# Experts in blocks of 32 slots, four side by side on TensorE, with the overflow blocks fetched by bounded row numbers on GpSimd's queue

## The reference, cut to what matters

```python
def hier_moe(h, router_g, router_g_b, router_e, router_e_b, w_gate, w_up, w_down):
    # 4 groups of 8 experts; each token takes the best group, and in it the best two experts
    ...
    for gi in range(N_EXPERT_GROUPS):
        hid = silu(einsum('td,edf->tef', xt, w_gate[gi])) * einsum('td,edf->tef', xt, w_up[gi])
        hid = hid * gates[:, gi, :, None]          # zero for the experts that a token does not take
        out = out + einsum('tef,efd->td', hid, w_down[gi])
```

## Time and profile before

| | |
|---|---|
| three runs | 3567.9, 3570.92, 3587.31 us, median 3570.92 |
| the profiled execution | 3579.16 us, span 3577.4, mean granted clock of PE 0.956 |
| busy in the span | PE 3245.1 us (91%), PEld 2503.2 (70%), DVE 1469.1 (41%), ACT 1129.8 (32%), POOL 220.7 (6%) |
| DMA | 623.97 MB, mean 174 GB/s; 494.01 MB on SP's queue, 126.46 MB on POOL's |
| transfers of expert weights | 234 on SP's queue |

### The profile page before, as it was taken

How to read it: one execution, slowest core, us unless ns; L and a number is a source line. 1 busy time by engine, 2 the same in 40 slices (tenths; PEclk the granted TensorE clock), 3 DMA queues, 4 the chain that set the end, 5 groups by cost and what they waited for, 6 DMA issues and landing times. The chain is left out here.

```text
span 3577.4 us, 54626 instructions
## 1 busy us (share of the span) xinstructions
PE 3245.1 (91%) x23980; PEld 2503.2 (70%) x23980; DVE 1469.1 (41%) x2737; ACT 1129.8 (32%) x1805; POOL 220.7 (6%) x370
## 2 busy tenths in 40 slices
PE   7888886999899689997999988999989998888898
PEld 5777675454698554545777766777767876777898
DVE  5455555222344642225323244333253334435554
ACT  4344443121343332113222223222232223224443
POOL 0122220000000000000000101000100000000000
PEclk8899897999999989998999989999999999999999
DMA  6433322999566049992453413444322222213452
GB/s 251 136 106 111 132 97 101 405 421 421 226 242 224 10 187 421 421 398 94 153 182 136 165 55 136 147 180 155 124 94 88 95 88 93 101 36 106 144 192 101
DMA packets 106718, 623.97 MB, mean 174 GB/s; under 512 B 11760, under 2 KB 14320, under 8 KB 48112
## 3 DMA queue, kind: packets, MB, share of 16 engines
q1 hardware_dynamic: 72208, 494.01, 36.1%
q0 software_dynamic: 34272, 126.46, 10.0%
HBM read 619.37 MB, written 1.05 MB: 173 GB/s over the span
## 5 line engine op out<-in xcount | busy, mean ns | idle before, releaser
L347 PE MATMUL ps<-t,t 128*128 128x512 f32 (+1 forms) x3488 | 1223.8, 351 | 113.0 <-DVE t L541 53.2
L348 PE MATMUL ps<-t,t 128*128 128x512 f32 (+1 forms) x3488 | 1212.4, 348 | 0.0
L349 PE MATMUL ps<-t,t 128*128 128x512 f32 (+1 forms) x3488 | 1211.0, 347 | 0.0
L324 DVE TENSOR_TENSOR t<-t,t 128x1024 fp32r<-128x1024 f32 x448 | 549.4, 1230 | 781.7 <-ACT t L305 781.6
L347 PEld LDWEIGHTS ps<-t,t 128*128 128x128 f32 x3488 | 669.3, 192 | 222.5 <-issue 70.3
L349 PEld LDWEIGHTS ps<-t,t 128*128 128x128 f32 x3488 | 669.3, 192 | 85.8
L348 PEld LDWEIGHTS ps<-t,t 128*128 128x128 f32 x3488 | 670.1, 192 | 81.6
L305 ACT ACTIVATE t<-t 128x1024 fp32r<-128x1024 f32 x448 | 469.6, 1054 | 590.0 <-PE ps L349 581.5
L1315 PE MATMUL ps<-t,t 128*64 128x512 f32 x1248 | 301.8, 597 | 8.8 <-DMA t<-in_experts_dram 8.8
L1315 PEld LDWEIGHTS ps<-t,t 128*64 128x64 f32 x1248 | 114.6, 137 | 187.2 <-issue 160.8
L679 POOL DMA_DIRECT2D t<-in_wmod_dram x224 | 118.5, 534 | 1855.9 <-PE ps L628 1738.4
(11 more groups left out here) (307 smaller groups left out, 3121.3 us busy)
## 6 DMA issues: line engine op xcount, KB each, us to landing
t<-in_experts_dram SPq DMA_DIRECT2D x234, 1024.0 KB, 13.5
t<-in_wall_dram SPq DMA_DIRECT2D x221, 1024.0 KB, 4.9
t<-in_wmod_dram POOLq DMA_DIRECT2D x224, 512.0 KB, 5.7
t<-in_wmod_dram SPq DMA_DIRECT2D x16, 512.0 KB, 13.1
t<-in_wall_dram SPq DMA_DIRECT2D x10, 512.0 KB, 3.6
t<-in_lora_dram POOLq DMA_DIRECT2D x8, 512.0 KB, 4.0
t<-in_rcst_dram POOLq DMA_DIRECT2D x1, 1536.0 KB, 6.4
t<-in_x_dram SPq DMA_DIRECT2D x1, 1024.0 KB, 8.1
```

The lines of the kernel that those rows point to most:

```text
L324: e.tensor_tensor(lo, self.raw(n), hi, ALU.subtract).then_inc(*net.wlo.up((self.name, n)))
L347: e.matmul(out, lh, rh, start=start, stop=False, **kw)
L348: e.matmul(out, lh, rl, start=False, stop=False, **kw)
L349: return e.matmul(out, ll, rh, start=False, stop=stop, **kw)
```

## The change

A block has 32 slots, four blocks make a **quad**, and there are 12 quads: near quads 0 to 7 (experts 4q to 4q+3) and far quads 8 to 11 with fifteen far blocks, 32 to 46, since more can be beyond 32 than beyond 64. They are worked on in the order 0, 1, 8, 2, 3, 9, 4, 5, 10, 6, 11, 7 (`ORDER`). PE works on a quad's four blocks side by side, in 32 columns each. Gate and up are done in two halves with other work between, and down of a quad comes behind the first half of the next. The gather is for two quads at a time, 256 columns.

The near transfers stay on SP's queue. `MORE` is 6 instead of 4: the first ten transfers have ten rooms, and after that the near ones go round six (the ring and t_143, t_144). The far blocks have t_139 to t_142 for their own. They are fetched on POOL's queue by `indirect_dma_start`: for each of the 128 partitions DVE has worked out a row number of the expert array (384 per expert), and a row number above the bound is dropped without an error. For a far block that holds nothing the counted expert is 32, whose rows are all above the bound. `min(…, 31)` and `fetch_ids` are gone.

```diff
+MORE = 6
...
+            self.rooms[NS + j], self.turn[NS + j], self.gates[NS + j] = ap, len(self.slots) - 1 + (j + 1) / (MORE + 1), stage
...
-    PAIRS = 20
-    BLOCKS = 39
+    ORDER = (0, 1, 8, 2, 3, 9, 4, 5, 10, 6, 11, 7)
+    QUADS = 12
+    BLOCKS = 47
...
+        turns = [(m, s) for n in range(self.QUADS + 1) for m, s in ((n, 0), (n - 1, 2), (n, 1)) if 0 <= m < self.QUADS]
+        near = 0
+        for n, s in turns:
+            for t, x in enumerate(self.blocks(n)):
+                key = ("moe", layer, "weights", n, s)
+                if x >= 32:
+                    self.w[n, t, s] = net.drawn_slot(t, more[t], ("block", x - 32, s), net.sums, key)
+                else:
+                    if near == NS + MORE:
+                        net.fewer_rooms(4, MORE - 4)
+                    self.w[n, t, s] = net.slot(("expert", 96 * layer + 3 * x + s), SW, net.sums, key)
+                    near += 1
...
+    def pe_gate_up(self, e, w, n, s):
...
+        for k in range(4 * s, 4 * s + 4):
...
+            for t in range(len(self.blocks(n))):
+                w.wait_ge(*net.landed(self.w[n, t, s]))
+                c = 128 * (n % 2) + 32 * t
+                m = e.matmul(net.ps[32 * t:32 * t + 32, b, :], self.Ug[g % 2][:, k, c:c + 32],
+                             net.ring_at(self.w[n, t, s])[:, 512 * (k % 4):512 * (k % 4) + 512], start=(k == 0), stop=(k == 7))
+        m.then_inc(*self.up(net.sums, "weights", n, s))
...
+        for n in range(self.QUADS):
+            g, kk = n // 2 + 1, 2 * (n % 2)
+            self.pe_gate_up(e, w, n, 0)
+            if n:
+                self.pe_down(e, w, n - 1)
+            if g < 6:
+                self.pe_gather(e, w, g, kk, 3)
+            if n:
+                self.pe_scatter(e, w, n - 1)
...
+            self.pe_gate_up(e, w, n, 1)
+            if g < 6:
+                self.pe_gather(e, w, g, kk + 1, 3)
...
+            self.pe_turn(e, w, n, 3 if g < 6 else 0)
...
+        for n in range(self.QUADS):
+            if self.ORDER[n] < 8:
+                continue
+            for s in range(3):
+                for t in range(len(self.blocks(n))):
+                    room, ap, _, _, (_, x, _), (marks, key), _ = net.slots[self.w[n, t, s]]
+                    w.wait_ge(*marks.of(key))
+                    e.indirect_dma_start(ap, None, rows, bass.IndirectOffsetOnAxis(ap=self.ids[:, 3 * x + s:3 * x + s + 1], axis=0),
+                                         bounds_check=12288 * self.l + 12287, oob_is_err=False).then_inc(net.s_drawn[t], 16)
```

More of the change, by code:

```diff
@@ L724, in __init__ @@
         self.rooms = {x: self.ring[:, SW * x:SW * x + SW] for x in range(NS)}
-        self.turn, self.filled, self.freed, self.gates = [x - NS for x in range(NS)] + [0] * NS, [0] * (2 * NS), {}, {}
+        self.turn, self.filled, self.freed, self.gates = [x - NS for x in range(NS)] + [0] * MORE, [0] * (NS + MORE), {}, {}
+        self.drawn = [0] * 4
         self.cst = self.take(NC_)
@@ L814, in more_rooms, with drawn_slot, fewer_rooms @@
         for j, ap in enumerate(aps):
-            self.rooms[NS + j], self.turn[NS + j], self.gates[NS + j] = ap, len(self.slots) + j, stage
-    def fewer_rooms(self):
-        self.rooms = {x: self.rooms[x] for x in range(NS)}
+            self.rooms[NS + j], self.turn[NS + j], self.gates[NS + j] = ap, len(self.slots) - 1 + (j + 1) / (MORE + 1), stage
+    def drawn_slot(self, x, ap, what, marks, key):
+        i, room = len(self.slots), NS + x
+        self.slots.append((room, ap, self.drawn[x], SW, what, self.freed[room], None))
+        self.drawn[x] += 1
+        self.freed[room] = (marks, key)
+        return i
+    def fewer_rooms(self, first=0, n=0):
+        self.rooms = {x: ap for x, ap in self.rooms.items() if x < NS or NS + first <= x < NS + first + n}
     def ring_at(self, i):
@@ L1215, in __init__ @@
         net.top = net.arena
-        more = [f(SW) for _ in range(4)]
+        more = [f(SW) for _ in range(MORE)]
         self.Uf = net.XW[:, :, 256:512]
@@ L1252, in __init__, with blocks, rows @@
         self.w = {}
[L1253 to L1257, removed]
-        net.fewer_rooms()
[L1260 to L1270, removed]
+        turns = [(m, s) for n in range(self.QUADS + 1) for m, s in ((n, 0), (n - 1, 2), (n, 1)) if 0 <= m < self.QUADS]
[5 more added lines that the diff above has]
+                    self.w[n, t, s] = net.drawn_slot(t, more[t], ("block", x - 32, s), net.sums, key)
+                else:
+                    if near == NS + MORE:
+                        net.fewer_rooms(4, MORE - 4)
+                    self.w[n, t, s] = net.slot(("expert", 96 * layer + 3 * x + s), SW, net.sums, key)
+                    near += 1
+        net.fewer_rooms()
+    def blocks(self, n):
+        q = self.ORDER[n]
+        return [x for x in range(4 * q, 4 * q + 4) if x < self.BLOCKS]
+    def rows(self, n):
+        return slice(0, 32 * len(self.blocks(n)))
     def c(self, name):
@@ L1299, in pe_gather @@
         w.wait_ge(*self.of(net.vecs, "tokens low"))
[L1300 to L1318, removed]
@@ L1320, in pe_turn @@
-    def pe_turn(self, e, w, p):
-        net, n = self.net, 64 * len(self.blocks(p))
-        b = self.take(w, 0, "turn", p)
-        w.wait_ge(*self.of(net.vecs, "hidden", p))
+        for j in range(2):
+            f = slice(256 * kk + 128 * j, 256 * kk + 128 * j + 128)
+            out = net.ps[:, b, 256 * j:256 * j + 256]
+            for i in range(2):
+                e.matmul(out, self.Uth[:, i, f], G[:, i, :], start=(i == 0), stop=False)
+                m = e.matmul(out, self.Utl[:, i, f], G[:, i, :], start=False, stop=(i == 1))
@@ L1433, in act, with act_down @@
+        self.emptied(net.acts, ("gather", g, kk), "gather", g, kk)
+    def act_down(self, e, w, n):
+        net, r = self.net, self.rows(n)
+        w.wait_ge(*self.of(net.sums, "weights", n, 2))
+        e.activation(self.Yh[r, :], net.ps[r, 1:3, :], ACT.Copy).then_inc(*self.up(net.acts, "down high", n))
     def act(self, e, w):
@@ L1559, in dve_choice @@
[L1559 to L1566 removed]
+            w.wait_ge(*self.of(net.sums, "gather", g - 2, 3))
```

274 lines of the change are left out of this document (146 added, 128 removed).

## The result

The changed kernel takes 3539.24 us (median of 4, 3533.29 to 3544.3), the kernel before 3577.18 beside it: a ratio of 0.9893, interval 0.9856 to 0.9929. So it is faster, by 38 us and not by the 75 forecast; the direction was right and the size was not. The profiled executions differ by 45.9 us (3577.4 to 3531.5 of span).

A forecast was written before the change was run, and what follows sets the result against it. It took PE and DMA to be equally full in the two MoE loops. Loops of 271 us gain 33 and 36, plus 2 x 3 ahead of them: 75 us less, 3496 against the median, range 3460 to 3530 (60%).

The forecast's parts named there:

- Bounds now: Two MoE loops, 304.1 and 306.9 us: PE and DMA both full, 14.9 us a pair each, so both must shrink.
- Bytes: Transfers per layer: 117 before (291 us), 96 after (239 us), because far blocks hold nothing and their dropped rows move nothing.
- PE four side by side: Matmuls in the loops: four blocks take about as long as two, 3.5 us a group, 14.8 a quad, 178 a loop.
- The group of near transfers: Four rooms released by one increment, six near rooms: 11.0 or 13.0 us a group, mean 12.0, 21.5 groups, 258 us.
- rival (b): Low clock in every near group: 14.5 us a group, 324 a loop, kernel slower at 3602 us; chance 9%.
- Pool: Far-room loads: four issues of 0.9 us plus 2.4 to landing, 6.0; 0.5 us open four times, 2 a loop.
- Rival (c): Pool's issues are dear, x us each: 3554 us at x = 2.0, 3624 at 3.1; chance 13%.
- Head and ahead of the loop: Loop start: ten transfers already there, first group 3.5 us; ahead of it, halved gather columns save about 3 us per layer.
- Tail: Loop end: from the last landing through down to the end of the scatter, 7.2 us.
- Sum: Loop 271 us, gains 33 and 36, plus 2 x 3 ahead of the loops: 75 us in all.

The follow-up runs named there:

- n4: The kernel before with its seven far blocks not fetched and PE's instructions the same: 3569.3 us, ratio 0.9984 to the kernel before.
- n2: The changed kernel without Pool's transfers, near stream going round all ten rooms, far matmuls reading the resident x: 3421.7 us, ratio 0.956 to the kernel before.
- n1: The changed kernel without Pool's 90 indirect transfers, far matmuls reading what the rooms last held, six near rooms kept: 3512.9 us, ratio 0.9818 to the kernel before.
- n10: The changed kernel with the old order of rooms at a layer's start, so six further rooms are not filled first: 3563.3 us, ratio 0.9956 to the kernel before.
- n5: The changed kernel with 384 taken off the far blocks' row numbers, so unused blocks really move rows: 3812.7 us, ratio 1.0655 to the kernel before.
- n3: The changed kernel with near transfers cut into 512 KB halves, each group of four halves released separately, Pool's transfers kept: 3527.1 us, ratio 0.9851 to the kernel before.
- n6: The changed kernel with near transfers in 512 KB halves and no transfers on Pool's queue: 3461.1 us, ratio 0.9676 to the kernel before.
- n7: The changed kernel with near transfers in halves and Pool branching over its transfers when no far block is in use: 3453.4 us, ratio 0.9653 to the kernel before.

## Why the prediction was right or wrong

**Bounds now: right.** Both engines had to be relieved; n4 shows that fewer bytes alone are not enough. The other half, a shorter PE alone, was not tried.

**Bytes: right.** SP's queue fell from 494.01 to 449.96 MB, 42 transfers of 1.0486 MB, and with ten rooms they pass at 2.55 us each (10.2 a group). Nothing of the far blocks moved.

**PE four side by side: right.** 32 records take 3.64 us at the full clock in the timeline (at 780.76, for one), 3.5 forecast (half of the timeline's 7.3; by the 0.242 us a record that the prediction has beside it, two blocks would take 7.7 and not 7.3), and PE's work in the loops fell from 296 to 234 us although most groups wait. The 178 us that the prediction added up for PE are not reached: even in n2 PE is busy 202.

**The group of near transfers: right in form, the term too small, and the larger part of the miss.** Without Pool (n1) the loops give (283.2 - 10.7) / 21.5 = 12.7 and 12.4 us a group for 12.0. With 21.5 groups a loop that is 23 us over the two loops (561.2 for 538). The clock was put well: of the 28 groups that stand in n1's timeline behind a wait for a near transfer, 15 took 4.7 to 6.6 us for their matmuls and the others 3.6 or less, as the prediction's half and half; the granted clock of n1's loops is 0.90 and 0.93. The rule of the Trainium skill that every burst shorter than the DMA wait ahead of it starts at the low clock ("TensorE: Matmul & The Clock Gate", HAM oscillation — how this bites in real kernels) agrees with these 15 of 28 groups and no more; fully applied it was rival (b), 14.5 us a group, and no loop has that. What the 12.0 left out seem to be late landings: the third and fourth matmul sets of the group shown lie 3.84 us apart for 2.49. In the trace's packet records one of the sixteen DMA engines finished 0.6 to 1.5 us behind the fifteen others in ten groups of n1's layer 0, 11.5 us in all, and in nine of the ten a 16 KB packet of code (0.9 to 1.0 us on one engine) had started 2 to 4 us earlier. These 11.5 us are most of the 14 that this loop is over its 269. With ten rooms the same late packets are there (up to 1.5 us behind the others in n2) and the group still takes 10.2 us, so a full queue seems to hide what a queue that runs dry in each group pays. This was read from records and not tested; whether the packets of code are the cause stays open.

**Pool: the step whose working failed.** I took 0.9 us an issue, a release-to-landing of 6.0 us, 0.5 us open at each of four places, 2 us a loop. n1 puts the price at 8.9 a loop, 17.8 for both (26 by the medians). The 6.0 was too small in three places. An issue takes 0.99 us, but four in a row come 1.30 apart, and the first comes 0.8 us or more after the release. A group that found the DMA engines idle shows both:

```profile
675.60 3.62 PE L1336 MATMUL ps<-t,t 128*32 128x512 f32 x26 [0.64 <-DMA t<-in_experts_dram,t]
680.01 0.99 POOL L1742 DMA_INDIRECT t<-in_experts_dram,t  x1 [9.11 <-PE ps L1336]
...
683.89 0.99 POOL L1742 DMA_INDIRECT t<-in_experts_dram,t  x1 [0.30 <-issue]
```

PE is done at 679.2, the fourth issue follows at 683.9 and lands 2.1 us later: 6.8 us for 6.0, with nothing in the way. The third place is the landing, because often something is in the way: the same order of releases frees near rooms and far rooms side by side. Of the 66 transfers whose landing the semaphore records give in full, 22 found the DMA engines less than 30% busy with near packets until they landed, and took 2.1 us from issue to landing (median; 3.5 at most). Another 35 found them at least 70% busy, and took 3.3 to 7.7, median 5.5. I had added the 2.4 us of an idle queue. What I should have asked is what stands ahead of a transfer on the DMA engines, not only on Pool's instruction queue; that the packets were to be tiny made me put the way at its shortest. Rival (c) named Pool's waits with a dear issue as the cause. It cannot be ruled out as a part: its own formula with x = 1.30 gives 4 x (2 x (5.2 + 2.4) - 13) = 8.8 us a loop, which is the size measured. No run parts the two, spacing and late landings; the wait to 770.73 above, where the fourth transfer was issued at 762.96, needs the late landing. None of the 90 issues took over 1.30 us. The Trainium skill's five times longer Pool DMA beside a DVE copy ("SBUF — State Buffer", A bandwidth-pool intuition that's wrong) shows in no issue here: three direct transfers were issued beside a DVE copy and took 0.58 us at most, and none of the indirect ones was.

**Head and ahead of the loop: right.** 6.6 us for 6 ahead of the loops; n10 gives the transfers fetched ahead at 24 us.

**Tail: small miss.** From the last landing at about 901.8 to the end of the last scatter are 9.4 us in layer 0 and 8.5 in layer 1, forecast 7.2. The last down of layer 0 takes 5.86 us where before it took 3.65; the granted clock is 0.61 during it, and was 0.50 in the 4.7 us ahead of it, in which PE was busy 1.9:

```profile
901.79 5.86 PE L1358 MATMUL ps<-t,t 128*32 128x512 f32 x26 [2.06 <-DMA t<-in_experts_dram]
908.76 2.47 PE L1374 MATMUL ps<-t,t 128*128 128x256 f32 x16 [1.11 <-ACT t L1462]
```

**Sum.** The direction was right; two terms of the sum were too small. Loops 579.0 for 542: 37 us short, 23 from the near groups (12.0 us a group, 12.7 and 12.4 measured, the tail in it) and 14 from Pool (2 us a loop, 8.9 measured). The medians are 37 apart as well, 75 to 38, and that agreement is partly chance: the profiled executions differ by 45.9, because of the 7.3 us outside that no term had. What neither term shows is that they are coupled: in the kernel as it stands the near stream's six rooms and Pool's late packets cover for each other, so that mending one gives 12 or 26 us and mending both 86.

## What to carry to other kernels

When a change takes two full engines down to neither full, count the buffers: by these runs, a group that is released by one increment wants behind its last landing as many rooms in flight as its own work and the way to the next landing take. With Pool's transfers out of the way, eight rooms or the same six in halves were worth more here (88 and 52 us) than the whole change (38). A transfer that moves nothing is not free if someone waits for it behind bulk transfers; if it is seldom needed, branch over it. And try two suspected waits together as well as each alone before writing either off.

## What the runs showed of the hardware

- An indirect transfer of 128 rows costs Pool 0.99 us (984/990/1299 ns), and four in a row come 1.30 us apart; a direct one 0.53.
- All its rows dropped, it still sends packets: those under 512 B are 24048 in the changed kernel and 12528 in n5, where the same rows move, and the difference of 11520 is 90 transfers of 128 rows. It lands 2.1 to 7.7 us after its issue, 2.1 in the median on nearly idle DMA engines and 5.5 on busy ones. Beside a queue that is full for more of the time (n3) PE's waits for it more than doubled, 28.1 to 64.9 us.
- The page's total of bytes read from HBM counts dropped rows as if they had moved: 669.79 MB with and without them. The bytes of the queue (126.60 and 220.93 MB) tell the truth.
- Transfers of 512 KB in rows of 4 KB, in stretches where the queue does not run dry (n3, n6, n7): 402 to 412 GB/s at a DMA share of 1.02 to 1.03 (once 384 in 20 us of n7). Of 1 MB in rows of 8 KB (n2): 419 to 422 at 1.01 to 1.02. Size and row length changed together.
